# A fifth seven-product pair in a hybrid-attention decoder block: the projections of heads seven and eight join the merge gates

## The reference

```python
h = rmsnorm(x, g_norm)
z = einsum('bsd,dn->bsn', h, w_in)
qa, ka, va, ga, qb, kb, vb, gb, fl, ma, mb = split(z)   # 8 heads each of branch a and b
oa = rmsnorm(diff_attention(rope(qa), rope(ka), va, lam)) * (1 - lam_init) * silu(ga)
ob = forgetting_attention(qb, kb, vb, cumsum(log_sigmoid(fl + b_f))) * silu(gb)
m  = sigmoid(ma) * (oa @ w_proj_a) + sigmoid(mb) * (ob @ w_proj_b)
out = rmsnorm(x + m @ w_out, g_final)
```

## Time and profile before

| | |
|---|---|
| median of 3 runs | 736.4 us (736.11 to 737.38) |
| the profiled execution | 736.15 us, its span 734.0 us |
| TensorE (PE) busy | 724.2 us, 99% |
| TensorE weight loads (PEld) | 604.3 us, 82% |
| VectorE (DVE) busy | 588.9 us, 80% |
| ScalarE (ACT) busy | 450.0 us, 61% |
| GpSimd (POOL) busy | 88.3 us, 12% |
| granted TensorE clock | 0.998 |
| DMA | 172.10 MB, mean 234 GB/s |

### The profile page before, as it was taken

The page is one execution under the profiler, slowest core; times in us unless marked ns, Lnnn a source line. Parts: engine busy times, 40 slices in busy tenths (PEclk is TensorE's granted clock), DMA queues, the critical chain, the costliest instruction groups (busy, mean ns, idle before and its releaser), DMA issues.

```text
span 734.0 us, 9419 instructions
## 1 busy us (share of the span) xinstructions
PE 724.2 (99%) x3478; PEld 604.3 (82%) x3478; DVE 588.9 (80%) x753; ACT 450.0 (61%) x668; POOL 88.3 (12%) x105
## 2 busy tenths in 40 slices
...
GB/s 337 209 233 312 144 229 207 247 226 243 331 182 232 214 265 210 269 302 185 215 261 200 251 258 292 173 285 198 231 248 241 211 190 201 279 230 236 288 199 115
DMA packets 48093, 172.10 MB, mean 234 GB/s; under 512 B 5352, under 2 KB 5360, under 8 KB 47536
## 3 DMA queue, kind: packets, MB, share of 16 engines
...
q0 software_dynamic: 256, 1.54, 0.6%
...
HBM read 169.37 MB, written 2.11 MB: 234 GB/s over the span
## 4 chain that ended last, share of the span: by engine, by line
PE 97%; DMA 1%; issue 1%; ACT 0%; DVE 0%; SPq 0%; DVEq 0%; POOLq 0%; POOL 0%
PE Z L401 28%; PE Z L402 28%; PE Z L416 21%; PE Z L469 7%; PE Z L576 3%; PE A L517 1%; PE A L483 1%; DMA w_raw<-in_w_main 1%; PE B L499 1%; PE Dk L508 1%; PE B L496 1%; PE A L680 0%; PE A L402 0%; PE A L401 0%; PE C L526 0%
## 5 line engine op out<-in xcount | busy, mean ns | idle before, releaser
L935 DVE TENSOR_TENSOR w_lo<-w_raw,w_hi 128x1024 fp32r<-128x1024 f32 (+1 forms) x242 | 296.4, 1231 | 87.0 <-ACT w_hi L702 85.9
L702 ACT ACTIVATE w_hi<-w_raw 128x1024 fp32r<-128x1024 f32 (+1 forms) x241 | 250.0, 1044 | 176.4 <-PE Z L416 132.7
L401 PE MATMUL Z<-w_hi,hT_hi 128*128 128x512 f32 (+2 forms) x680 | 257.5, 382 | 0.0
L402 PE MATMUL Z<-w_hi,hT_lo 128*128 128x512 f32 (+2 forms) x680 | 255.8, 379 | 0.0
L401 PEld LDWEIGHTS Z<-w_hi,hT_hi 128*128 128x128 f32 x680 | 127.8, 188 | 24.6
L402 PEld LDWEIGHTS Z<-w_hi,hT_lo 128*128 128x128 f32 x680 | 127.8, 188 | 23.4
L416 PE MATMUL Z<-w_lo,hT_hi 128*128 128x512 f32 (+2 forms) x576 | 146.5, 377 | 0.0
L416 PEld LDWEIGHTS Z<-w_lo,hT_hi 128*128 128x128 f32 x576 | 104.6, 188 | 19.9
L702 ACT ACTIVATE w_hi<-x_and_g 128x1024 fp32r<-128x1024 f32 x72 | 76.3, 1059 | 58.9 <-DVE x_and_g L950 33.9
L935 DVE TENSOR_TENSOR w_lo<-x_and_g,w_hi 128x1024 fp32r<-128x1024 f32 x72 | 90.0, 1252 | 26.9 <-ACT w_hi L702 25.7
L401 PE MATMUL Z<-w_hi,sum_hi 128*128 128x512 f32 x260 | 102.8, 396 | 0.0
...
## 6 DMA issues: line engine op xcount, KB each, us to landing
w_raw<-in_w_main SPq DMA_DIRECT2D x287, 512.0 KB, 4.2
x_and_g<-in_w_main SPq DMA_DIRECT2D x18, 512.0 KB, 6.5
...
```

What stands on the lines that cost most here:

```text
L401: pe.matmul(acc, a_hi, b_hi, start=first, stop=False)
L402: pe.matmul(acc, a_lo, b_hi, start=False, stop=False)
L702: act.activation(w_hi[:, t % RING, 0:cols_of(t)], weights(t), ACT.Copy).then_inc(hi_ready, 1)
L935: dve.tensor_tensor(w_lo[:, t % RING, 0:n], weights(t), w_hi[:, t % RING, 0:n].bitcast(fp32), ALU.subtract).then_inc(lo_ready, 1)
```

## The change

`GROUPS` becomes 5 and the new first group's column chunks are heads 6 and 7 (`PAIR_HEADS`) instead of two gate chunks. Their 16 plain tiles are gone, and 28 short jobs take their place. Eleven heads are left to the chunks; each chunk now has 20 jobs, eight plain tiles and twelve short ones, and the last eight short jobs (of now 140) stay where they were. The whole line has 326 jobs. The heads of the pair land in the place of the third gate group (`z_of`), where ScalarE scales them in place (`gate_in_place`), and their attention reads them there; the four gate groups follow, and the third writes that place only after both heads are done. The attention keeps its order of heads; its jobs are 20 apart for the first three heads of the chunks and 16 apart after that. All banks and counters are renumbered. The diff, cut to its core:

```diff
--- before.py
+++ after.py
@@ -26,7 +26,8 @@
 Z_SLOTS = 3
 FL_COLS = 2 * HD + HEADS
 SLOT = 2 * CHUNK
-GROUPS, FORMS, QUARTERS = 4, 7, 4
+GATE_GROUPS, GROUPS, FORMS, QUARTERS = 4, 5, 7, 4
+PAIR_HEADS, PAIR_GROUP = (6, 7), 2
 P1, P5, P6, P3, P7, P4, P2 = range(FORMS)
 SUM_1, SUM_2, SUM_4, SUM_3 = range(4)
 SPLIT_HEADS = 13
@@ -36,14 +37,17 @@
 MERGE, PROJ, OUT = N_HEADS, N_HEADS + 8, N_HEADS + 12
 
 FL_JOB, VG_JOB, PLAIN_JOB, MIXED_JOB = 8, 16, 20, 28
-FOX_JOB = MIXED_JOB + 16 * (N_HEADS - 3)
+ALONE = [h for h in range(N_HEADS) if h not in PAIR_HEADS]
+MIXED = 20
+FOX_JOB = MIXED_JOB + MIXED * (len(ALONE) - 3)
 FOX2_JOB = FOX_JOB + 16
 DIFF_JOB = FOX2_JOB + 8
 OUT_JOB = DIFF_JOB + 16
 LAST_JOB = OUT_JOB + 30
 JOBS = LAST_JOB + TILES
 
-HEAD_STEPS, SUM_STEPS = (0, 2, 4, 6, 8, 10, 12, 13), (1, 3, 5, 7, 9, 11, 14, 15)
+HEAD_STEPS = (0, 3, 5, 8, 10, 13, 15, 17)
+SUM_STEPS = [u for u in range(MIXED) if u not in HEAD_STEPS]
 FOX_STEPS, FOX_SUM_STEPS = (0, 2, 4, 5, 8, 11, 14, 15), (1, 3, 6, 7, 9, 10, 12, 13)
 OUT_PLAIN = [(2, j) for j in range(TILES)] + [(0, j) for j in range(4, TILES)] + [(1, j) for j in range(4, TILES)]
 SUMS_BEHIND = [0, 0, 0, 2, 1, 1, 1, 1, 1, 1, 1, 1, 1, 1, 1, 1]
@@ -51,26 +55,29 @@
 OUT_OF = {OUT_JOB + u: kind for u, kind in enumerate(OUT_ORDER) if kind != "s"}
 OUT_PLACE = {2: 0, 0: 1, 1: 2}
 OUT_DONE = {2: 0, 1: 1, 0: 2}
-SUM_JOB = ([MIXED_JOB + 16 * c + u for c in range(N_HEADS - 3) for u in SUM_STEPS] + [FOX_JOB + u for u in FOX_SUM_STEPS]
+SUM_JOB = ([MIXED_JOB + MIXED * c + u for c in range(len(ALONE) - 3) for u in SUM_STEPS] + [FOX_JOB + u for u in FOX_SUM_STEPS]
            + [OUT_JOB + u for u, kind in enumerate(OUT_ORDER) if kind == "s"])
 SUM_OF = {job: s for s, job in enumerate(SUM_JOB)}
-X_AT = {21: 0, 28: 1, 38: 2, **{MIXED_JOB + 16 * (b - 2) + 4: b for b in range(3, N_HEADS)},
-        FOX2_JOB + 1: N_HEADS, DIFF_JOB + 1: N_HEADS + 1}
-Y_AT = {25: 0, 33: 1, 43: 2, **{MIXED_JOB + 16 * (b - 2) + 9: b for b in range(3, N_HEADS)}, FOX2_JOB + 5: N_HEADS}
+X_ALONE = {**{3 + c: MIXED_JOB + MIXED * (c + 1) + 4 for c in range(3)},
+           **{b: MIXED_JOB + 3 * MIXED + 4 + 16 * (b - 5) for b in range(6, N_HEADS)}}
+X_AT = {21: 0, 28: 1, 38: 2, **{job: b for b, job in X_ALONE.items()}, FOX2_JOB + 1: N_HEADS, DIFF_JOB + 1: N_HEADS + 1}
+Y_AT = {25: 0, 33: 1, 43: 2, **{job + 5: b for b, job in X_ALONE.items()}, FOX2_JOB + 5: N_HEADS}
 
 C_ZERO, C_MASK, C_TRI, C_IDENT, C_ONE = 0, P, 2 * P, 3 * P, 4 * P
 C_COS, C_SIN, C_BF, C_GS, C_LAM = 5 * P, 5 * P + 16, 5 * P + 32, 5 * P + 40, 5 * P + 41
 C_ALL = C_LAM + 4 * QK
 
 
-def fill_of(c):
+def fill_of(h):
+    c = ALONE.index(h)
     return c if c < 2 else c + 1
 
 
-def head_job(c, j):
+def head_job(h, j):
+    c = ALONE.index(h)
     if c == 0:
         return j
-    return PLAIN_JOB + j if c == 2 else MIXED_JOB + 16 * (c - 3) + HEAD_STEPS[j]
+    return PLAIN_JOB + j if c == 2 else MIXED_JOB + MIXED * (c - 3) + HEAD_STEPS[j]
 
 
 def max_count(heads):
@@ -86,8 +93,8 @@
 
 
 PARTS_AT = {PLAIN_JOB + 7: 0, MIXED_JOB + 2: 1, MIXED_JOB + 11: 2, MIXED_JOB + 18: 3}
-O_SPLIT_AT = {FOX_JOB - 20: 0, FOX_JOB - 14: 1, FOX2_JOB + 3: 2, FOX2_JOB + 4: 3}
-HEAD_OF = {head_job(c, j): (c, j) for c in range(2, N_HEADS) for j in range(TILES)}
+O_SPLIT_AT = {FOX_JOB - 20: 0, FOX_JOB - 11: 1, FOX2_JOB + 3: 2, FOX2_JOB + 4: 3}
+HEAD_OF = {head_job(c, j): (c, j) for c in ALONE[2:] for j in range(TILES)}
 FOX_OF = {fox_job(n, j): (n, j) for n in range(4) for j in range(4)}
 DIFF_OF = {diff_job(n, j): (n, j) for n in range(4) for j in range(4)}
 
...
@@ -231,7 +238,7 @@
         square_out = z_sb[:, 2]
         gates_flat = gates[:].rearrange("p g m b n -> p (g m b n)")
         rows = gates_flat[:, 3 * D_MODEL:4 * D_MODEL]
-        sums_raw = gates_flat[:, D_MODEL:3 * D_MODEL].rearrange("p (f k n) -> p f k n", f=4, k=TILES)
+        sums_raw = gates_flat[:, 0:2 * D_MODEL].rearrange("p (f k n) -> p f k n", f=4, k=TILES)
         y_sb = gates_flat[:, 0:2 * D_MODEL].rearrange("p (m n) -> p m n", m=M_TILES)
         yg = gates_flat[:, 2 * D_MODEL:4 * D_MODEL].rearrange("p (m n) -> p m n", m=M_TILES)
         oT_hi = sum_hi[:].rearrange("p f k n -> p (f k n)").rearrange("p (h n) -> p h n", h=N_HEADS)
@@ -304,8 +311,20 @@
 
         def blocks_of(g):
             if g < GROUPS:
-                return [gates[:, g, m, branch, :] for m in range(M_TILES) for branch in range(2)]
+                return [gates[:, PAIR_GROUP if g == 0 else g - 1, m, branch, :] for m in range(M_TILES) for branch in range(2)]
             return [y_sb[:, m, branch * CHUNK:(branch + 1) * CHUNK] for m in range(M_TILES) for branch in range(2)]
+
+        def z_of(h):
+            if h in PAIR_HEADS:
+                return gates[:, PAIR_GROUP, :, PAIR_HEADS.index(h), :]
+            return z_sb[:, ALONE.index(h) % Z_SLOTS]
+
+        def wait_z(engine, h):
+            if h in PAIR_HEADS:
+                engine.wait_ge(pair_ready, 4)
+            else:
+                engine.wait_ge(evac[0], fill_of(h) + 1)
+                engine.wait_ge(evac[1], fill_of(h) + 1)
 
         def form_bank(g, f):
             if g < GROUPS:
@@ -336,9 +355,9 @@
                     if g == GROUPS:
                         n, half = {P1: (0, 0), P5: (1, 0), P6: (1, 1), P3: (1, 1), P7: (0, 0), P4: (0, 1), P2: (0, 1)}[f]
                         return w_main[8 * (OUT + n) + 2 * half + q - 4]
-                    c, half = {P1: (MERGE, 0), P5: (MERGE + 4, 0), P6: (MERGE + 4, 1), P3: (MERGE + 4, 1), P7: (MERGE, 0),
-                               P4: (MERGE, 1), P2: (MERGE, 1)}[f]
-                    return w_main[8 * (c + g) + 4 * half + q - 4]
+                    n, half = {P1: (0, 0), P5: (1, 0), P6: (1, 1), P3: (1, 1), P7: (0, 0), P4: (0, 1), P2: (0, 1)}[f]
+                    c = PAIR_HEADS[n] if g == 0 else MERGE + 4 * n + g - 1
+                    return w_main[8 * c + 4 * half + q - 4]
                 if job in FOX_OF:
                     n, j = FOX_OF[job]
                     return w_main[8 * (PROJ + n) + j]
...
@@ -814,7 +831,7 @@
 
             def o_hi_part(i):
                 heads = slice(4 * i, min(4 * i + 4, SPLIT_HEADS))
-                act.wait_ge(w_used, SUM_JOB[3 * FORMS * QUARTERS + 4 * (P5 + i) + 3] + 1)
+                act.wait_ge(w_used, SUM_JOB[(GROUPS - 1) * FORMS * QUARTERS + 4 * (P5 + i) + 3] + 1)
                 act.wait_ge(oT_hi_ready, heads.stop)
                 act.activation(oT_hi[:, heads, :], o_T[:, heads, :], ACT.Copy).then_inc(o_hi_split, 1)
 
@@ -825,8 +842,12 @@
             def gate_in_place(g, f):
                 m, branch = {P3: (0, 1), P7: (1, 1), P4: (1, 0), P2: (0, 0)}[f]
                 act.wait_ge(folded, 5 * g + f - 1)
-                act.activation(gates[:, g, m, branch, :], gates[:, g, m, branch, :], ACT.Tanh,
-                               scale=half_rstd[:, m:m + 1]).then_inc(gates_ready, 1)
+                if g == 0:
+                    z_block = z_of(PAIR_HEADS[branch])[:, m]
+                    act.activation(z_block, z_block, ACT.Copy, scale=rstd[:, m:m + 1]).then_inc(pair_ready, 1)
+                else:
+                    act.activation(gates[:, g - 1, m, branch, :], gates[:, g - 1, m, branch, :], ACT.Tanh,
+                                   scale=half_rstd[:, m:m + 1]).then_inc(gates_ready, 1)
 
             def attention(job):
 
...
```

47 lines of the change are left out of this document (22 added, 25 removed).

## The result

The changed kernel takes **740.34 us** (median of 9 runs, 738.82 to 742.58) where the kernel before takes 736.4 us: a ratio of 1.0052 (95% interval 1.0038 to 1.0066). It is slower by 3.9 us, and 731.3 us was predicted. The profiled execution took 740.3 us, its span 738.5 us, 4.5 us above the 734.0 us of before.

A forecast was written before the change was run, and what follows sets the result against it. TensorE's matmuls were taken to bound the kernel: 736.15 us of the profiled execution - 5.44 saved + 0.3 of stalls = 731.0, with 0.25 more for the median of the runs 731.3 us; range 730.6 to 734.3 us.

The forecast's parts named there:

- Term 1: TensorE's matmuls: 192 taken out, 168 put in, 24 fewer at 0.2267 us each, 5.44 us saved on the path.
- Term 2, size of the work: VectorE's extra work: 12 `w_lo`, 16 subtractions and 7 folds come in, 36.7 us.
- None goes under zero: At the thin places among the chunks `w_lo` still comes before TensorE needs it; 0.3 us of stalls in all.
- the thin place with head 8: Head 10's last plain tile meets head 8's scores, then subtractions: `w_lo` lead 1.2 us, some 0.8 after correction.
- Averages: VectorE's share of TensorE's time among branch-a heads rises from 81% to 90%: on average hidden, half the reserve gone.
- Edits costed at nothing: ScalarE's extra work, evacuations, bank folding, 12 loads and moved attention were all taken as covered, adding no time.
- Rival B: Late loads find the `w_lo` lead thin and stop TensorE, 0.9 to 3.6 us of stalls, say 733.2 us; chance 0.22.
- Rival C: Loads into `w_raw` become the bound, landing at 6.2 us and costing 0.2 us a round: 742 us; chance 0.04.
- Rival D: VectorE stalls take the gain: ten stretches of subtractions each stop TensorE half a us, 736.0 us; chance 0.06.
- The signs: TensorE's busy time falls 5.4 us, matmul starts stay 0.227 us apart, VectorE some 86%, smallest leads 0 to 2 us.

The follow-up runs named there:

- e1: The changed kernel with its 88 weight subtractions on VectorE cut to one column each, written to a scratch tile: 731.39 us, ratio 0.9933 to the kernel before.
- e13: The changed kernel with five slots of `w_raw` in place of four, room coming from shared scratch tiles: 733.3 us, ratio 0.9959 to the kernel before.

## Why the prediction was wrong

- **Term 1** was right: 24 matmuls, 5.44 us. Prices of 1.36 and 2.72 us stand, and e1, whose profiled span is 5.0 us below before, has nearly the whole gain.
- **Term 2, size of the work**: right, 36.0 us for 36.7.
- **Term 2, "None goes under zero"**: this step failed, 9.9 us of stalls where 0.3 was taken. The count itself was good to some half a us at its place: 1.2 us of lead was worked out for the thin place with head 8 (0.8 after the correction), 1.3 to 1.4 was measured (jobs 159 to 161), and TensorE did not stop there. But it summed instructions from a fresh start at an evacuation. It had no term for what VectorE has already lost when it enters a stretch, and a wait of 1.4 or 1.8 us for a load, or of 4.35 us for GpSimd's bias, carried along, is more than the lead. The trace of before had ten such waits for loads, 8.4 us, and one of 2.7 us for the bias; I looked at the longest wait for a load alone. The last columns of the table are the case that I had not counted at all.
- **Averages**: 81 to 90% was read as a reserve that is smaller but enough. The reserve is what makes a delay good, and it is not spread evenly. In the earlier trace rows VectorE is full for a few us and then free; now it is full for 16 us and, ahead of head 14, for over 30, so that the leads of one stretch are what the stretch before left over.
- **Edits costed at nothing**: the evacuation "would show if ScalarE came late by more than 1.4 us". It did so twice (1.74 and 1.13 us); the cover of 2.72 us was right, and what stood ahead of it in ScalarE's queue, the exponentials and through them VectorE, was not priced. Nor was VectorE's own gate product at job 256 (1.58 us), behind two `w_lo` and two smaller instructions.
- **Rival B** named the mechanism, a late load finding the lead thin, with "two or so" events and 0.22. Its number was too small, and so was its price of 1.3 us: five places lost 1.1 to 2.4 us each, since a lateness stops TensorE at one job after another. That "a slot is freed late" stood there as an argument; that it comes round again and is carried for tens of us did not. **Rival C** had the nearest time, 742, with 0.04, and by luck: landing was 4.3 us, 242 GB/s in the mean, and e1, with the same loads, has no stall. Its round was averaged over four jobs; where VectorE runs through `w_lo` after `w_lo` it comes back to a slot sooner than a load lands (2.8 against 4.6 us at 518). **Rival D**, 736.0 with 0.06, had VectorE's stalls as its mechanism, spread over ten stretches; they were five places and twice as dear.
- **The signs**: VectorE's share (85%) and the spacing of 0.227 us came as announced, the smallest leads (0.05 us) lay inside the announced 0 to 2 us and so told nothing, and the rows of `PEld` waiting for `w_lo` were named as the sign of "wrong". TensorE's busy time was a bad sign to name, since it counts some 5 us of the stalled time as work: 723.9 with stalls, 719.0 in e13 without.
